# Sparse attention of a one-core Trainium2 kernel: 64 units in one stream, with wide and narrow query tiles in turn

## The reference, cut to what matters

```python
def one_block(args):                       # 128 queries
    ...
    _, idx = lax.top_k(score, k_sel)       # k_sel = 256, causal
    c_sel = jax.vmap(lambda c, i: c[i])(c_kv, idx)
    dist = tq[None, :, None] - idx
    bias = jnp.moveaxis(rel_bias[relative_bucket(dist)], -1, 2)
    logits = jnp.einsum('bqhc,bqkc->bqhk', qa, c_sel).astype(jnp.float32) * (DSA_DH ** -0.5)
    logits = jnp.where((dist >= 0)[:, :, None, :], logits + bias.astype(jnp.float32), -1e30)
    p = jax.nn.softmax(logits, axis=-1).astype(c_sel.dtype)
    return jnp.einsum('bqhk,bqkc->bqhc', p, c_sel)
...
q_abs = jnp.einsum('bshd,hdc->bshc', q_d, w_uk[l])
o_lat = dsa_sparse_attention(q_abs, c_kv, q_idx, w_idx, k_idx, rel_bias)
o_dsa = jnp.einsum('bshc,hcd->bshd', o_lat, w_uv[l])
```

## Time and profile before

| | |
|---|---|
| median of 3 runs | 4184.12 us (4177.09 to 4186.31) |
| span of the profiled execution | 4180.0 us |
| what lies around the span, by the median | 4.1 us |
| busy share of the span: PE, DVE, ACT, POOL | 83%, 49%, 26%, 28% |
| mean granted TensorE clock | 0.916 |
| bias, latent-turning and sparse stages | 428.5 to 816.3 us |

### The profile page before, as it was taken

How to read it: one execution, slowest core, us unless ns; L and a number is a source line. 1 busy time by engine, 2 the same in 40 slices (tenths; PEclk the granted TensorE clock), 3 DMA queues, 4 the chain that set the end, 5 groups by cost and what they waited for, 6 DMA issues and landing times. The chain is left out here.

```text
span 4180.0 us, 48490 instructions
## 1 busy us (share of the span) xinstructions
PE 3465.1 (83%) x18422; PEld 2694.9 (64%) x18422; DVE 2061.5 (49%) x3428; ACT 1105.4 (26%) x1958; POOL 1185.2 (28%) x670
## 2 busy tenths in 40 slices
PE   6697677669985877799999984999988878998978
PEld 4376455549864666678787873766655766675657
DVE  3699587876543334363545447033355340333553
ACT  2444233323312111200000013033345221333540
POOL 2122122214334343453443521321020333111012
PEclk8799799869987988899999996999999989998999
DMA  3010000000021111131212202110000221000011
GB/s 102 26 36 25 16 3 4 0 7 1 1 81 49 32 43 35 54 129 62 95 60 91 78 23 67 46 27 26 1 16 1 81 85 38 21 21 13 4 61 65
DMA packets 227765, 169.82 MB, mean 41 GB/s; under 512 B 42216, under 2 KB 214832, under 8 KB 226832
## 3 DMA queue, kind: packets, MB, share of 16 engines
q1 hardware_dynamic: 225008, 166.77, 13.0%
q10 hardware_dynamic: 2592, 0.81, 0.1%
HBM read 150.63 MB, written 16.92 MB: 40 GB/s over the span
## 5 line engine op out<-in xcount | busy, mean ns | idle before, releaser
L1443 DVE TENSOR_TENSOR I-13702S<-I-13702S,c_causal 128x256 f32<-128x256 f32 x64 | 27.7, 432 | 457.8 <-PE I-13702S L1381 457.8
L773 DVE TENSOR_TENSOR I-11268act_f<-I-11267act_g,I-11274p_u 128x512 f32<-128x512 f32 x44 | 28.3, 684 | 258.1 <-PE I-11274p_u L268 258.1
L873 DVE SCALAR_TENSOR_TENSOR y_T<-y_T 128x1024 f32<-128x1024 f32 x48 | 140.2, 2971 | 5.4 <-DMA y_T<-in_w_ada 5.4
L759 ACT ACTIVATE I-11267act_g<-I-11273p_g 128x1024 f32<-128x1024 f32 x22 | 22.6, 1028 | 422.0 <-PE I-11273p_g L268 422.0
L264 PE MATMUL I-11273p_g<-hf_hi,I-11249w_hi 128*128 128x512 f32 x352 | 109.5, 392 | 5.0 <-POOL hf_lo L482 5.0
L266 PE MATMUL I-11273p_g<-hf_lo,I-11249w_hi 128*128 128x512 f32 x352 | 109.3, 392 | 0.0
L268 PE MATMUL I-11273p_g<-hf_hi,I-11251w_lo 128*128 128x512 f32 x352 | 109.1, 392 | 0.0
L268 PE MATMUL I-11274p_u<-hf_hi,I-11252w_lo 128*128 128x512 f32 x352 | 108.4, 389 | 0.0
L264 PE MATMUL I-11274p_u<-hf_hi,I-11250w_hi 128*128 128x512 f32 x352 | 108.4, 389 | 0.0
L266 PE MATMUL I-11274p_u<-hf_lo,I-11250w_hi 128*128 128x512 f32 x352 | 108.4, 389 | 0.0
L1323 POOL TENSOR_TENSOR I-13692w_hi<-I-13690w_raw,c_ones 128x1024 fp32r<-128x1024 f32 x16 | 30.3, 1892 | 268.8 <-PE I-13706half L1334 189.9
(11 more groups left out here) (1115 smaller groups left out, 10375.6 us busy)
## 6 DMA issues: line engine op xcount, KB each, us to landing
y_T<-in_w_ada SPq DMA_DIRECT2D x48, 512.0 KB, 3.3
saved_x<-x_T SPq DMA_DIRECT2D x3, 4096.0 KB, 13.7
x_T<-saved_x SPq DMA_DIRECT2D x3, 4096.0 KB, 15.1
I-11247w_raw<-in_w_gate SPq DMA_DIRECT2D x22, 512.0 KB, 4.5
I-11248w_raw<-in_w_up SPq DMA_DIRECT2D x22, 512.0 KB, 4.3
I-13690w_raw<-in_w_in SPq DMA_DIRECT2D x16, 512.0 KB, 3.8
I-13691w_raw<-in_w_in SPq DMA_DIRECT2D x14, 512.0 KB, 3.8
I-11261d_raw<-in_w_down SPq DMA_DIRECT2D x11, 512.0 KB, 5.0
```

Of the source, the lines that this page charges most:

```text
L773: nc.vector.tensor_tensor(act_f[:, cols], act_g[:, cols], p_u[:, h, :], ALU.mult).then_inc(product, 1)
L873: self.nc.vector.scalar_tensor_tensor(out=self.raw[s], in0=self.raw[s], scalar=1.0, in1=self.c_row, op0=ALU.mult, op1=ALU.mult, accum_out= ...
L1443: self.nc.vector.tensor_tensor(diag, diag, tiled(self.mask, 2), ALU.add).then_inc(self.masked, 1)
```

## The change

`sparse_stage` is written anew as one straight stream of 64 units without a loop or a seam between pairs:
- Order of tiles within a head: 7, 0, 6, 1, 5, 2, 4, 3.
- The run-ahead is two units; two score buffers `S`, three `probs`, three `grid`; `PT` is two banks used in turn by groups of four blocks, even groups copied by VectorE, odd ones by ScalarE.
- The mask is kept as bf16 and added by TensorE (an identity in bf16 times the mask), the band is two f32r parts (high and low) in place of one f32; the far bias is no longer added.
- VectorE's `to_grid_of` adds the rounding constant while it reads PSUM and takes the maximum in the same instruction; VectorE forms the rest, GpSimd's subtraction is gone. The division goes to ScalarE.
- Projection, absorb, turning and w_uv product of the pairs become 56 side steps of 512 columns, most of them one after a unit, with their own PSUM bank; ScalarE copies all their results.
- `bias_stage` and `turn_latents_stage` are gone: the lookup goes to `key_index_stage`, the turning of the latents to the head of `sparse_stage`.

The order and the side steps:

```diff
+    ORDER = [7, 0, 6, 1, 5, 2, 4, 3]
...
+        def aux_at(u):
+            i, r = divmod(u, 2 * NT)
+            if r in (1, 2):
+                return (("turn", "value")[r - 1], i - 1, 3) if i > 0 else None
+            if r in (5, 9, 13):
+                return "turn", i, (r - 5) // GROUP
+            if r in (6, 10, 14):
+                return "value", i, (r - 6) // GROUP
+            if r in (3, 4) and i + 1 < PAIRS:
+                return "project", i + 1, r - 3
+            if r in (7, 8, 11, 12) and i + 1 < PAIRS:
+                return "absorb", i + 1, (7, 8, 11, 12).index(r)
```

On TensorE, the scores of unit u and the list of the stream:

```diff
+                    if u > 1:
+                        pe.wait_ge(rest_done, u - 1)
...
+                        mm(out_u[:, h, 0:b - a], q, c_T[:, a:b], start=True, stop=False)
...
+                            for part in band:
+                                mm(out_u[:, h, near - a:b - a], flip_r[:, :], part[:, 2 * i + head, at:at + b - near].bitcast(F32R), start=False, stop=False)
+                        last = mm(out_u[:, h, 0:b - a], unit_b[:, :], mask(t)[:, a:b], start=False, stop=True)
...
+                scores(0)
+                scores(1)
+                for u in range(UNITS):
+                    if u + 2 < UNITS:
+                        scores(u + 2)
+                    turn(u)
+                    if u > 0:
+                        values(u - 1)
+                    aux_step(u)
```

On ScalarE:

```diff
+                exponentials(0)
+                for u in range(UNITS):
+                    if u + 1 < UNITS:
+                        exponentials(u + 1)
+                    copy_turned(u)
+                    if u > 0:
+                        divide(u - 1)
+                    found = aux_at(u)
+                    if found is not None:
+                        aux_copy(*found)
```

On VectorE, `to_grid_of(u)` and the list:

```diff
+                    v.tensor_scalar(shift, src, GRID_ROUND, TAKEN, ALU.add, ALU.max, accum_out=top[:, one]).then_inc(shifted, 1)
+                    dve.wait_ge(shifted, u + 1)
+                    v.tensor_scalar(part, shift, GRID_ROUND, GRID / 2, ALU.subtract, ALU.add).then_inc(gridded, 1)
+                    v.tensor_scalar(neg[:, one], top[:, one], GRID_ROUND, -1.0, ALU.subtract, ALU.mult).then_inc(bias_set, 1)
+                    dve.wait_ge(gridded, u + 1)
+                    v.scalar_tensor_tensor(out=shift, in0=shift, scalar=GRID_ROUND, in1=src, op0=ALU.subtract, op1=ALU.subtract).then_inc(rest_done, 1)
...
+                to_grid_of(0)
+                to_grid_of(1)
+                for u in range(UNITS):
+                    multiply(u)
+                    if u + 2 < UNITS:
+                        to_grid_of(u + 2)
+                    copy_turned(u)
+                    invert(u)
```

In `key_index_stage` two transfers, one matmul, three VectorE operations on 8 rows and two stores are added:

```diff
+                nc.tensor.matmul(p_rows[0:H8, 0:HANKEL], table[:, :], bucket[:, :], start=True, stop=True).then_inc(looked_up, 1)
...
+                less_far(nc.vector.tensor_scalar(rows[:, :], p_rows[0:H8, 0:HANKEL], p_rows[0:H8, 0:1], None, ALU.subtract))
+                less_far(nc.vector.tensor_copy(rows_hi[:, :], rows[:, :]))
+                less_far(nc.vector.tensor_tensor(rows_lo[:, :], rows[:, :], rows_hi[:, :].bitcast(F32), ALU.subtract))
```

In `index_stage` the masks are written as bf16, and those of tiles 0 and 1 are copied:

```diff
+                for t in range(SELECT_FROM):
+                    own(v.tensor_copy(masks(t), scores(t)))
...
-                    own(v.tensor_scalar(scores(t), scores(t), 0.0, MASKED, ALU.is_gt, ALU.mult))
+                    own(v.tensor_scalar(masks(t), scores(t), 0.0, MASKED, ALU.is_gt, ALU.mult))
```

More of the change, by code:

```diff
@@ L81 @@
 M_DB, M_DA, M_WIX = IDX_DIM, IDX_DIM + DN_HEADS, IDX_DIM + 2 * DN_HEADS
-MASKED = -1e30
+MASKED = -2.0 ** 100
 TAKEN = -3e38
@@ new lines, in turn @@
+                def turn(u):
+                    t, before = unit(u)[2], groups_before(u)
+                    pe.wait_ge(probs_ready, u + 1)
+                    if u == 0:
+                        pe.wait_ge(aux_out, FRONT)
+                        pe.wait_ge(latents_out, 1)
+                    for g in range(groups(u)):
+                        b, n = (before + g) % 2, (before + g) // 2
+                        wait(pe, copied[b], n)
+                        for k in range(GROUP * g, min(GROUP * (g + 1), t + 1)):
+                            last = nc.tensor.transpose(PT[b][:, k % GROUP * P:(k % GROUP + 1) * P], probs[u % 3][:, k * P:(k + 1) * P], ident)
+                        last.then_inc(turned, 1)
@@ new lines, in values @@
+                def values(u):
+                    t, after = unit(u)[2], groups_before(u + 1)
+                    pe.wait_ge(copied[0], (after + 1) // 2)
+                    wait(pe, copied[1], after // 2)
+                    wait(pe, o_out, u)
+                    for k in range(t + 1):
+                        last = mm(O[:, u % GROUP, :], probs_T[u % 2][:, k, :], c_tok[:, k, :], start=(k == 0), stop=(k == t))
+                    last.then_inc(o_done, 1)
+                project(0, 0)
+                project(0, 1)
@@ L2152, in turn_latents_stage @@
[L2152 to L2167 removed]
+                v = nc.vector
```

368 lines of the change are left out of this document (234 added, 134 removed).

## The result

The changed kernel takes 4083.1 us (median of 4 runs, 4077.1 to 4090.7) against 4182.4 us (4 runs, 4177.1 to 4186.3): ratio 0.976, 95% interval 0.974 to 0.978. That is 99 us less, where 84 were forecast. The profiled execution has a span of 4075.3 us against 4180.0.

The account below looks back on a forecast made before the run. Bound by VectorE's list inside a pair, drains between pairs and GpSimd's collisions with the product; first T 451.5 + 266.9 + tail 13.5 ends the stage at 731.9 instead of 816.3, 84.4 us less: 4100 us, range 4066 to 4132.

Parts of the forecast that it names:

- the chain: Sparse stage: VectorE's list to the narrow product, then TensorE's to the next wide scores; 266.9 us for 30 couples with waits.
- the first T: Start of the sparse stream: moment when a wide unit's scores (u+2) are first done; 451.5, bounds 450 and 453.
- the tail: End of the sparse stage: last grid, turns, values, division, turn out, values out, with copies; 13.5 us.
- Lead-in: Ahead of the sparse stream: bias and turning stages go, 17.2 us earlier; first scores 13.5 us after first transfer, at 442.
- the upper case: Start of the sparse stream: scores(2) take 4.2 us at the lower TensorE clock rather than 2.1.
- The table lookup: Moved into the key-index stage, hidden beside TensorE and ScalarE; costs nothing, without that cover 2 us.
- The unpriced matmuls: TensorE's scores: 128-column f32r taken as 0.08 us; bf16 mask 0.43 at 1024 columns, bounds 0.2 to 0.9.
- 53 in the sum: VectorE's summed work in the sparse stage: 26.6 us per head, 53 us a pair where it was 72.
- Rival A: Sparse stage: TensorE alone is the bound, 7.8 us a couple, 33 us less than forecast; 4067, chance 0.12.
- Rival B: Sparse stage: units keep their old pace, only lead-in and three 15 us seams are won, 62 us; 4122, chance 0.16.
- Rival C: Sparse stage: run-ahead of two isn't enough, late ScalarE makes engines take turns; +87 us, 4271, break-even 11.7 a couple, chance 0.04.
- Rival E: VectorE's product runs at half rate even without GpSimd beside it; 11 us more than forecast, 4111, chance 0.02.

Follow-up runs that it names:

- no_mask: Changed kernel without the bf16 matmuls that add the mask to the scores; 4074.9 us (one run), stage 276.7 us against 288.0.
- max_back: Changed kernel with the row maximum made by a VectorE pass of its own over the shifted scores; 4119.8 us (one run), stage 324.3 us against 288.0.
- divide_back: Changed kernel with the division of the 64 output blocks moved from ScalarE back to VectorE; 4091.9 us (one run), stage 295.9 us against 288.0.
- seams_back: Changed kernel with the run-ahead stopped at each of the three pair ends; 4102.4 us (one run), stage 305.1 us against 288.0.
- turn_first: Changed kernel with the turn of u ahead of the scores of u+2 in TensorE's queue; 4174.7 us (one run), stage 380.9 us against 288.0.
- before_sub: Kernel before the change, with GpSimd's subtraction in the sparse stage made by VectorE; 4179.3 us (one run), stage 388.7 us against 387.8.

## Why the prediction was right, and where it was off

*The time.* 4100 forecast, 4083.1 measured, inside the range. The direction and the mechanism held; two terms of the sum were too large, both on the chain. By the trace the stage ended 15.2 us before the forecast's 731.9: 0.6 at the first T and 17.0 on the chain, less 2.4 in the tail.

*Lead-in: right in the sum, by two misses that nearly cancel.* First scores forecast for 442, they came at 440.4, 1.8 us sooner after the first transfer than the 13.5 that I took. From there to the first T it took 10.6 us and not 9.5, since the scores of the next wide unit ran at the lower clock, which I had named as the upper case: 4.3 us (446.34 to 450.69), behind a wait of 2.84 us. So the first T, forecast for 451.5, came at 450.9. The window of after around it, as above:

```profile
440.00:450.00 10.00, 6.71 (x18) 3.60 (x20) 5.06 (x11) 5.09 (x8) 1.34 (x2) 0.78 0.06 16
```

The table lookup in the key-index stage cost nothing, as argued: the next stage's first transfer is at 145.40, before it was at 145.75.

*The chain: right, two sizes off.* Between first and last T I had 266.9 us and the trace has 249.9. The 0.3 us a couple for waits between groups in TensorE's queue (9 us in all) was not needed: after each hand-over TensorE's groups follow without a gap (514.28, 514.77, 515.89). The other 8 us are the grid pass, 0.27 us a couple: 3.14, 2.80, 2.46 and 2.13 us for tiles 7 to 4, where I had 3.41, 3.07, 2.74 and 2.41. I took 1.28 us from the old pass and then 0.12 for the accumulator read and the wait on top; in the trace the new pass takes 1.23 us, and the read at 511.29 begins before that has ended. The other terms differ by as much, but cancel: copy and hand-over to the turn are 4 us below the forecast over the 30 couples (VectorE to TensorE takes 0.06 us here, 514.22 to 514.28, where I had 0.23), and turns, values, side work and scores are 4 us above. In the couple 4/3 of a first head (9.34 us, forecast 9.32) the shorter pass is offset by the steps behind the turn, as its timeline of TensorE shows: values 1.21 us (start to start) where I had 1.12, absorb 1.05 where I had 0.86.

```profile
548.21 1.28 PE L2228 MATMUL I-2935O<-x_T,I-2925probs_T 128*128 128x128 f32 x10
549.42 1.12 PE L2162 MATMUL I-2936aux<-x_T,I-2905w_uk 64*128 64x512 f32 x2
550.47 1.99 PE L2200 MATMUL I-2931S<-x_T,I-2917q_abs 128*128 128x512 f32 x4
```

The unpriced matmuls were near their values: 0.11 to 0.15 us for a 128-column f32r matmul (I had 0.08), 0.22 for 512 columns of the bf16 mask (0.215). no_mask gives the mask's worth on the chain, 11 us.

*Tail: short by 2.4.* 13.5 forecast, 700.83 to 716.68 is 15.9.

*VectorE: 49 us a pair, against 53 in the sum*; product 1213 ns at 1024 columns. The prediction's 1.1 ns a column for the product at 896 leaves out the fixed part: 1.08 us are 1.2 ns a column.

*Rival A (TensorE alone is the bound)* did not come: TensorE still waits 22 us for narrow products, and max_back and divide_back lengthen most couples by the VectorE work that was put on its wide half. But the couples near it are many. Where the wait for a narrow product vanishes (tiles 5/2), TensorE's own list sets the couple, by a hair: in the couple from 569.67 the product ends at 573.01 and the turn starts at 573.15, behind the mask.

*Rival B* had the right worry and the wrong size. The hand-over is 0.06 us to TensorE and 0.2 back, the clock stays at 1.00 from 503 on, the masks are cheap. Its seams (15 us each) would have been 45 us: seams_back gives 17.1 for the stopped run-ahead alone. max_back shows that the clock part is near: with waits of 2.3 to 2.9 us instead of 1.3 the granted clock falls now and then.

*Rival C* is a real mechanism with about the price that it was given (+87 against before): turn_first makes the engines take turns on purpose, by TensorE's order and not by a late ScalarE, and loses 92.9 us against after. Its couples of 10.2 to 12.3 us lie around the 11.7 that I had as the break-even, and turn_first indeed ends near the kernel before. In after it didn't come: no row of waits names ScalarE for the wide products except one of 1.8 us.

*Rival E (the product at half rate)*, which was the rule of the Trainium skill's page "Vector Engine (DVE) Microarchitecture Reference", section 7, is refuted for this form: 1024 f32 columns from two SBUF tensors with an accumulator take 1213 to 1220 ns in after and 1217 in before_sub, where GpSimd has no part in the softmax.

*Where the 99.8 us come from.* Ahead of the first scores 19.5 (31.2 before, 11.7 after, from the timelines). The others were measured alone, by putting one thing back: separate maximum 36.3 (some 7 of them with the lower clock), stopped run-ahead at the seams 17.1, GpSimd beside VectorE 8.9, division on VectorE 7.9. Against that stand 9.2 lost by the alternation and 11.3 paid for adding the mask by TensorE. The gains sum to 89.7 and the losses to 20.5, so some 30 us of the gain have no single part here. Candidates without an experiment are projection and absorb, which stood between the pairs (VectorE stood 8.2 us at each of three starts of a pair), the order of the queues against before's, fewer copies of turned blocks and TensorE's waits for them, and the f32r band. The parts also share one chain, so they need not add up, and the 8.9 is neither the price of before's longer GpSimd instructions nor net of the subtraction that VectorE now makes.

## What to carry to other kernels

In a loop in which two engines take turns, find in each half of a couple which list ends last: work put on the other list there is free, and work on this one counts to the full (max_back: some 1.1 us of pass, 1.11 us of couple). A balanced-looking alternation of wide and narrow tiles is worth what the two halves say, here less than falling widths, and an order of tiles and products chosen by following both lists gave 25 us more than the one in the change (23.3 by the length: 13.7 for the order of the products, 9.6 for the order of the tiles on top of it; falling widths together with both products at once were not run). Test a run-ahead first by its place in the in-order queue: one swapped line was worth 93 us.

## What the runs showed of the hardware that I had not expected

- A VectorE instruction with its tensors in SBUF, started while a GpSimd tensor_tensor runs, ends just after GpSimd's: 0.94 us for a 128-column product that takes 0.27 alone, 0.96 for a 128-column grid pass that takes 0.23. An 896-column pass with PSUM as one source was not touched (1.09 us), and a 512-column product that started together with GpSimd's instruction kept its 0.67 us while GpSimd's took 1.81.
- The granted clock of TensorE fell to a mean of 0.76 to 0.87 in windows of max_back that follow waits of 2.3 to 2.9 us, while after's waits of 1.3 us left it at 1.00. Waits of 2.4 and 2.3 us left it at 1.00 too, in max_back from 505 to 682. The cause is open.
- An add and maximum pass with accumulator from PSUM takes 1225 ns at 1024 columns, no more than the plain pass beside it (1222), so a maximum made this way is free, where passes of their own cost 29 us by themselves and 36 with the lower clock.
